# Index logits of the sparse attention: two heads per step, as two 64-row products straight from the rotated tile

## The chip, the cores and the metric

One core of one Trainium2 chip runs the whole program. The metric is the device time of that core in microseconds, as the median of several executions: 2955.22 us over 3 runs (2954.88 to 2957.07).

## The reference, cut to what matters

Two transformer blocks in float32 on 16 + 512 tokens of width 1024. The second block begins with a sparse attention (`dsa_attention`), which picks for every query the 128 keys with the highest index score. Only the score is touched:

```
qi = rope(qi.reshape(B, T, IDX_HEADS, IDX_DIM), cos, sin)     # 8 heads of 64
ki = rope(ki[:, :, None, :], cos, sin)[:, :, 0, :]            # one key head of 64
logits = jnp.einsum('qhd,sd->qhs', qi_blk, ki_s)
score = jnp.einsum('qh,qhs->qs', w_blk, jax.nn.relu(logits))
score = jnp.where(causal, score, -jnp.inf)
_, idx = lax.top_k(score, topk)                               # topk = 128
```

So for each head there is a product of queries and keys over only 64 dimensions, then relu, then a sum over the 8 heads weighted per query.

## The kernel before, in words

Each engine runs its own program, written out by hand; semaphores order them. Tokens are cut into five tiles of 106 (the last of 104), `ROWS` and `ENDS`. Query tile 0 needs no scores, since it has under 128 keys. Query tile t (1 to 4) is scored against the keys 0 to `ENDS[t]`, which are 212, 318, 424 and 528 columns. `pieces` cuts the 528 into two products of 264, since a bank of PSUM holds 512.

The index queries are four tiles of `pf` (12 to 15), each with two heads of 64 rows: head 0 in the partitions 0 to 63 and head 1 in 64 to 127. Tile 16 of `pf` is the index key, with the same 64 rows in both halves (the weights are laid as `[ki, ki]`). All five are rotated in place while the stage `dsa_a` projects them.

The stage around the change comes between two runs of projections, `dsa_a` (8 blocks) and `dsa_b` (10 blocks), and goes through three engines:

- TensorE, `pe_dsa`, lines 1795 to 1810: 32 products, numbered n = 0 to 31. The outer loop is over the four query tiles m, then over the head hh, then over t, so four products of one head follow each other. The moving operand is the key tile with all 128 rows, and the stationary one is a copy of the query tile in which the other head's 64 rows are zero (`ix_zero`). Product n writes the banks 4 and 5 (n even) or 6 and 7 (n odd), and waits for `ix_act`, that is for the relu of product n - 2.
- ScalarE, `act_dsa`, lines 1869 to 1875: for each n the relu from PSUM into `ix_score[n % 2]`. It waits for `ix_pe` (product n) and for `ix_dve` (the sum of n - 2).
- VectorE, `dve_dsa`, lines 1995 to 2004: for each n one SCALAR_TENSOR_TENSOR, which adds the relu times the query's weight to `bias` of tile t. There is a drain ahead of every fourth one, since `bias` of the same t was written four instructions before.

GpSimd makes the copies (`apart`, lines 1908 to 1914): two copies of 64 rows for each query tile, the first two tiles' behind the last weight split of `dsa_a`, the third's and the fourth's when the products of tile m - 2 are through. The other halves were set to zero by four memsets at lines 1921 to 1923. Behind the copies in GpSimd's program stand two `rope_cosine` and then the weight splits of `dsa_b`.

What follows the stage: TensorE's two `spread` products and VectorE's two multiplies with them (line 2008), the rotation of the two key tiles of the attention (`rope_turn`, `rope_cosine`, `rope_sine` 5 and 6), and `dve_topk` on VectorE, sixteen rounds of MAX8 and MATCH_REPLACE8, beside which TensorE, ScalarE and GpSimd do `dsa_b`. A barrier of all engines stands before the attention.

Of the kernel before, what the change touches and what calls it, by code (L numbers as in the profile page):

```python
# [24 lines left out]
P = 128  # L25
# [3 lines left out]
T = NMETA + SEQ  # L29
HT = T // 2  # L30
C = 106
NCH = -(-T // C)
TS = NCH * C
ROWS = [min(C, T - t * C) for t in range(NCH)]
ENDS = [min(C * (t + 1), T) for t in range(NCH)]
# [78 lines left out]
def wait(e, sem, value):  # L114

    if isinstance(value, int) and value <= 0:
        return
    e.wait_ge(sem, value)
# [27 lines left out]
def pieces(n):  # L146

    return [(0, n)] if n <= 512 else [(0, HT), (HT, HT)]


def build_program(nc, io):
# [113 lines left out]
    tmp, half = dsb("free_l", "tmp", [64, 2 * BASE * BASE]), dsb("free_l", "half", [64, BASE * BASE // 4])  # L265
# [13 lines left out]
    pf = r2("pf", [P, 24 * T])  # L279
# [42 lines left out]
    ix_zero = ri("ix_zero", [P, 4, T])  # L322
# [16 lines left out]
    def sem(name):  # L339
        return nc.alloc_semaphore(name)  # L340
# [44 lines left out]
    q_out, q_sq, q_sum, q_turn, q_moved, q_done, q_table = map(sem, (  # L385
        "q_out", "q_square", "q_sum", "q_turned", "q_turned_out", "q_rotated", "q_tables"))
    q_arg, q_root, tok_out, v_turn = sem("q_argument"), sem("q_root"), sem("token_scale_out"), sem("v_turned_dsa")
    ix_q, ix_pe, ix_act, ix_dve = sem("index_q"), sem("index_logits"), sem("index_relu"), sem("index_added")
    f_sq, f_used, f_root, f_inv, f_spread, f_app = map(sem, (
        "fox_square", "fox_square_used", "fox_root", "fox_inverse", "fox_spread", "fox_normalized"))  # L390
    f_turn, f_vturn, f_vout = sem("fox_scale_turned"), sem("fox_v_turned"), sem("fox_v_stored")
# [44 lines left out]
    def tile_at(buf, m, n=T, off=0):  # L436
        step = TS if buf is qkv or buf is oacc else T
        return buf[:, bass.ds(m * step + off, n)]
# [1331 lines left out]
    def pe_dsa(pe):  # L1770
        a0, b0 = SEGS["dsa_a"].b0, SEGS["dsa_b"].b0
        pe.wait_ge(const2_in, 48)
        for j in range(8):
            products(pe, Blk(a0 + j, 0), xah, xal, KT, *((2, None, False, pe_sums(live=True, gained=True))
                                                         if j == 0 else ()))
            if 2 <= j <= 6:
                rope_turn(pe, j - 2)

        pe.wait_ge(rope_dve, 4)
        for c in range(NCH):  # L1780
            pe.transpose(ps[0:ROWS[c], 7, c * 8:(c + 1) * 8], wi[:, c * C:ENDS[c]], ident[0:8, 0:8])
        for c in range(NCH):
            mm = pe.matmul(ps[0:ROWS[c], 7, 64 + c:65 + c], rstd[0:1, c * C:ENDS[c]], ones[0:1, 0:1],
                           start=True, stop=True)
        mm.then_inc(wit_pe, 1)

        pe.wait_ge(rope_dve, 5)
        for m in range(2):
            pe.wait_ge(kn_sq, m + 1)
            for h in range(2):  # L1790
                mm = pe.matmul(ps[0:16, 4 + h, 0:HT], win64[:, 14 - 2 * m:30 - 2 * m],
                               cout[m][:, h * HT:(h + 1) * HT], start=(m == 0), stop=(m == 1))
        mm.then_inc(kn_sum, 1)

        for m in range(4):
            pe.wait_ge(ix_q, m + 1)
            for k in range(IX):
                hh, t = divmod(k, NCH - 1)
                t += 1
                n = m * IX + k  # L1800
                if n == 0:
                    pe.wait_ge(kn_root, 1)
                elif n == 1:
                    pe.wait_ge(tok_out, 1)
                else:
                    pe.wait_ge(ix_act, n - 1)
                for x, (o, c) in enumerate(pieces(ENDS[t])):
                    mm = pe.matmul(ps[0:ROWS[t], 4 + 2 * (n % 2) + x, 0:c], ix_zero[:, 2 * (m % 2) + hh, C * t:ENDS[t]],  # L1808
                                   pf[:, 16 * T + o:16 * T + o + c], start=True, stop=True)
                mm.then_inc(ix_pe, 1)  # L1810

        pe.wait_ge(kn_inv, 1)
        for m in range(2):
            pe.wait_ge(ix_act, 4 * IX - 1 + m)
            for h in range(2):
                mm = pe.matmul(ps[:, 4 + 2 * m + h, 0:HT], spread[:, m * P:(m + 1) * P], hinv[:, h * HT:(h + 1) * HT],
                               start=True, stop=True)
            mm.then_inc(kn_spread, 1)
        rope_turn(pe, 5)
        rope_turn(pe, 6)  # L1820

        def q_turned(m):
            wait(pe, q_moved, m)
            pe.wait_ge(q_out, m + 1)
            for h in range(2):
                mm = pe.matmul(bank(4 + h), rot_q[:, :], tile_at(pf, m, HT, h * HT), start=True, stop=True)
            mm.then_inc(q_turn, 1)
            pe.wait_ge(q_sq, m + 1)
            for c in range(NCH):
                mm = pe.matmul(ps[0:ROWS[c], 6, 16 * c + 2 * m:16 * c + 2 * m + 2], sq[m % 2][:, c * C:ENDS[c]],  # L1830
                               win64[:, 14:16], start=True, stop=True)
            mm.then_inc(q_sum, 1)

        for j in range(10):
            products(pe, Blk(b0 + j, 0), xah, xal, KT)
            if j == 1:
                pe.wait_ge(rope_dve, 7)
                pe.wait_ge(q_table, 1)
            if 1 <= j <= 8:
                q_turned(j - 1)  # L1840
        pe.wait_ge(q_moved, 8)
        for m in range(2):
            pe.wait_ge(q_out, 9 + m)
            for c in range(NCH):
                o = (ps[0:ROWS[c], 4 if m == 0 else 7, c * P:(c + 1) * P] if c < 4
                     else ps[0:ROWS[c], 5 if m == 0 else 2 * (b0 % 2), 0:P])
                at = (10 + m) * T + c * C
                mm = pe.transpose(o, pf[:, at:at + ROWS[c]], ident[:, :])
            mm.then_inc(v_turn, 1)

    def act_dsa(act):
# [15 lines left out]
        act.activation(two(hroot[0:16, :]), pair_of(4, 16), ACT.Sqrt, bias=eps[0:16, 0:1], scale=1.0 / 64  # L1867
                       ).then_inc(kn_root, 1)
        for n in range(4 * IX):
            t = n % (NCH - 1) + 1  # L1870
            w_, rows = ENDS[t], ROWS[t]
            act.wait_ge(ix_pe, n + 1)
            wait(act, ix_dve, n - 1)
            act.activation(as_psum(ix_score[n % 2][0:rows, 0:w_], w_), psum_cols(4 + 2 * (n % 2), rows, w_),
                           ACT.Relu).then_inc(ix_act, 1)
# [29 lines left out]
    def pool_dsa(pool):  # L1905
        a0, b0 = SEGS["dsa_a"].b0, SEGS["dsa_b"].b0

        def apart(m):
            x = tile_at(pf, 12 + m)
            wait(pool, ix_pe, (m - 1) * IX if m > 1 else 0)  # L1910
            pool.drain()
            pool.wait_ge(rope_dve, m + 1)
            pool.tensor_copy(ix_zero[0:64, 2 * (m % 2), :], x[0:64])
            pool.tensor_copy(ix_zero[64:P, 2 * (m % 2) + 1, :], x[64:P]).then_inc(ix_q, 1)

        for j in range(8):
            split_lo(pool, Blk(a0 + j + 1, 0))
            if j == 0:
                pool.wait_ge(const2_in, 48)
                pool.drain()  # L1920
                for i in range(0, 4, 2):
                    pool.memset(ix_zero[64:P, i, :], 0.0)
                    pool.memset(ix_zero[0:64, i + 1, :], 0.0)
                pool.drain()
            if 2 <= j <= 6:
                rope_cosine(pool, j - 2)
            if j == 7:
                apart(0)
                apart(1)
        apart(2)  # L1930
        apart(3)
        pool.drain()
        rope_cosine(pool, 5)
        rope_cosine(pool, 6)

        def q_rotated(m):
            x = tile_at(pf, m)
            t = ix_zero[:, m % 2, :]
            pool.wait_ge(q_moved, m + 1)
            if m == 0:  # L1940
                pool.wait_ge(q_table, 1)
            pool.tensor_tensor(t, t, cossin[:, 1, :], ALU.mult)
            pool.wait_ge(q_sq, m + 1)
            pool.tensor_tensor(x, x, cos_q[:, :], ALU.mult)
            pool.drain()
            pool.tensor_tensor(x, x, t, ALU.add).then_inc(q_done, 1)

        for j in range(10):
            split_lo(pool, Blk(b0 + j + 1, 0))
            if 2 <= j:  # L1950
                q_rotated(j - 2)
        pool.drain()
        zero_halves(pool)

    def dve_dsa(dve):
# [37 lines left out]
        dve.wait_ge(kn_root, 1)  # L1993
        dve.reciprocal(hinv[0:16, :], hroot[0:16, :]).then_inc(kn_inv, 1)
        for n in range(4 * IX):
            hh, t = divmod(n % IX, NCH - 1)
            t += 1
            if n % (NCH - 1) == 0:
                dve.drain()
            head = 2 * (n // IX) + hh  # L2000
            dve.wait_ge(ix_act, n + 1)
            dve.scalar_tensor_tensor(rows_of(bias, t), ix_score[n % 2][0:ROWS[t], 0:ENDS[t]],
                                     wit[0:ROWS[t], t, head:head + 1], rows_of(bias, t),
                                     ALU.mult, ALU.add).then_inc(ix_dve, 1)
        for m in range(2):
            dve.wait_ge(kn_spread, m + 1)
            x = tile_at(pf, 8 + m)
# [840 lines left out]
```

## Time and profile before

| | |
|---|---|
| median of 3 executions | 2955.22 us |
| span of the profiled execution | 2954.3 us (no other time of it is given; the median lies 0.9 us above) |
| TensorE busy | 2750.1 us, 93% of the span |
| VectorE busy | 1457.1 us, 49% |
| granted TensorE clock, mean over the span | 0.969 of full speed |
| first MATMUL to last sum of the index stage | 1515.14 to 1543.75 us |

A MATMUL's recorded time goes from its start until its last result is written, so consecutive ones overlap, and their spacing is shorter than their duration. float32 products run as two LDWEIGHTS and two MATMULs each; the profile has 80 MATMULs of line 1808 for 40 logical products (32, and 8 more because those of 528 columns are cut in two).

### The profile page before, as it was taken

The page shows a single profiled execution, that of the slowest core. Times are in us where ns is not written, and L with a number is a line of the kernel's source. Part 1 is how long each engine was busy: PE and PEld are TensorE (multiplying, and loading weights), DVE is VectorE, ACT ScalarE, POOL GpSimd, SP SyncE. Part 2 cuts the span into 40 slices and gives each one's busy share as a digit, 9 for nine tenths or more (in the row PEclk, how much of TensorE's full clock was granted, in tenths as well). Part 3 has the DMA queues.
Part 4 walks back from the last instruction along what each step waited for, and adds up shares of the span by engine and source line. Part 5 has one row for each costly group of instructions (what it writes and reads, how often), then busy time and mean ns, then how long its engine had stood idle before and what let it go on. Part 6 is the DMA issues. An engine that isn't in the chain of part 4 may idle for free.

```text
span 2954.3 us, 48212 instructions
## 1 busy us (share of the span) xinstructions
PE 2750.1 (93%) x17591; PEld 2406.2 (81%) x17591; DVE 1457.1 (49%) x2316; ACT 1021.6 (35%) x1759; POOL 1097.3 (37%) x588
## 2 busy tenths in 40 slices
PE   6986788889999999999899899999999999999998
PEld 6965788868987778888779679999998988877876
DVE  2664776743212663323679556345366224555433
ACT  4761222223243332222423563222233255422221
POOL 3422333314444444444447003444444310244443
PEclk8997988999999999999999999999999999999999
DMA  3210000012233333333212002232322200133332
GB/s 98 89 50 7 10 10 10 12 52 89 89 92 93 93 94 92 94 93 98 86 36 72 1 1 79 86 90 88 93 86 77 68 30 1 58 92 93 93 93 93
DMA packets 88859, 197.90 MB, mean 67 GB/s; under 512 B 38140, under 2 KB 40238, under 8 KB 88728
## 3 DMA queue, kind: packets, MB, share of 16 engines
q1 hardware_dynamic: 84964, 192.72, 22.0%
q10 hardware_dynamic: 3764, 3.38, 0.4%
q8 instruction: 88, 1.44, 0.2%
q14 instruction: 43, 0.35, 0.0%
HBM read 192.24 MB, written 3.82 MB: 66 GB/s over the span
## 4 chain that ended last, share of the span: by engine, by line
issue 44%; PE 17%; POOL 12%; DVE 4%; ACT 1%; POOLq 1%; DVEq 1%; ACTq 0%
POOL wl L479 12%; PE ps L515 9%; PE ps L2161 2%; PE ps L2192 2%; DVE work L2061 1%; DVE top L2058 1%; PE ps L1808 1%; PE ps L2179 1%; PE ps L2311 1%; PE ps L2320 1%; ACT prob L2230 0%; POOLq L129 0%; DVE rowmax L2261 0%; PE ps L890 0%; PE ps L2164 0%
## 5 line engine op out<-in xcount | busy, mean ns | idle before, releaser
L479 POOL TENSOR_TENSOR wl<-wraw,wh 128x1024 fp32r<-128x1024 f32 x353 | 876.3, 2483 | 1292.7 <-ACT wh L471 1292.6
L471 ACT ACTIVATE wh<-wraw 128x1024 fp32r<-128x1024 f32 x353 | 372.5, 1055 | 578.2 <-PE ps L515 490.3
L515 PE MATMUL ps<-xah,wh 128*128 128x264 f32 (+1 forms) x2672 | 500.5, 328 | 24.7 <-ACT xah L844 14.2
L515 PE MATMUL ps<-xah,wl 128*128 128x264 f32 (+1 forms) x2672 | 488.1, 323 | 0.0
L515 PE MATMUL ps<-xal,wh 128*128 128x264 f32 (+1 forms) x2672 | 486.6, 322 | 0.0
L515 PEld LDWEIGHTS ps<-xah,wh 128*128 128x128 f32 x2672 | 405.6, 189 | 78.7 <-issue 23.8
L515 PEld LDWEIGHTS ps<-xah,wl 128*128 128x128 f32 x2672 | 403.9, 189 | 41.3 <-issue 0.7
L515 PEld LDWEIGHTS ps<-xal,wh 128*128 128x128 f32 x2672 | 402.4, 188 | 40.7
L663 DVE TENSOR_TENSOR res<-res,stage 128x512 f32 (+3 forms) x112 | 81.8, 730 | 440.3 <-ACT stage L579 440.3
L515 PE MATMUL ps<-xbh,wh 128*128 128x264 f32 (+1 forms) x1392 | 274.7, 337 | 13.5 <-POOL wl L479 12.9
L515 PE MATMUL ps<-xbh,wl 128*128 128x264 f32 (+1 forms) x1392 | 270.0, 334 | 0.0
L515 PE MATMUL ps<-xbl,wh 128*128 128x264 f32 (+1 forms) x1392 | 269.5, 333 | 0.0
L515 PEld LDWEIGHTS ps<-xbh,wh 128*128 128x128 f32 x1392 | 218.2, 189 | 48.3 <-POOL wl L479 16.4
L579 ACT ACTIVATE stage<-ps 128x512 f32<-128x512 f32 (+1 forms) x136 | 81.9, 603 | 467.0 <-PE ps L515 466.9
L515 PEld LDWEIGHTS ps<-xbh,wl 128*128 128x128 f32 x1392 | 218.0, 189 | 27.4
L515 PEld LDWEIGHTS ps<-xbl,wh 128*128 128x128 f32 x1392 | 217.5, 188 | 27.4
L656 DVE TENSOR_SCALAR xbh<-stage 128x512 f32 (+3 forms) x102 | 144.7, 1419 | 18.2 <-issue 16.6
L2161 PE MATMUL ps<-pf,qz 128*104 128x264 f32 (+4 forms) x384 | 124.2, 410 | 24.7 <-ACT prob L2230 13.8
L2261 DVE TENSOR_REDUCE rowmax<-ps 106x1 f32<-106x106 f32 (+4 forms) x160 | 77.7, 488 | 126.5 <-PE ps L2166 70.4
L658 DVE TENSOR_TENSOR xbl<-stage,xbh 128x512 f32 (+3 forms) x102 | 116.4, 1141 | 15.3 <-issue 1.5
L1189 PE MATMUL ps<-xq,ob 106*106 106x106 f32 x480 | 64.8, 299 | 61.4 <-DVE xq L1485 41.7
L1189 PEld LDWEIGHTS ps<-xq,ob 106*106 106x106 f32 x480 | 60.1, 211 | 63.8 <-DVE xq L1485 43.4
(332 smaller groups left out, 3250.1 us busy)
## 6 DMA issues: line engine op xcount, KB each, us to landing
wraw<-in_w SPq DMA_DIRECT2D x353, 512.0 KB, 3.5
res<-in_x SPq DMA_DIRECT2D x4, 528.0 KB, 5.8
res<-in_x ACTq DMA_DIRECT2D x1, 2048.0 KB, 7.9
out<-res SPq DMA_DIRECT2D x1, 2048.0 KB, 6.9
block_in<-mt SPq DMA_DIRECT2D x120, 4.0 KB
xq<-block_out SPq DMA_DIRECT2D x120, 8.0 KB
block_out<-yy SPq DMA_DIRECT2D x20, 56.0 KB
cossin<-in_cossin ACTq DMA_DIRECT2D x1, 528.0 KB
```

The source lines that it names most:

```text
L471: act.activation(wh[:, s * DM:(s + 1) * DM], wraw[:, s * DM:(s + 1) * DM], ACT.Copy).then_inc(hi_done, 1)
L479: pool.tensor_tensor(wl[:, s * DM:(s + 1) * DM], wraw[:, s * DM:(s + 1) * DM], wh[:, s * DM:(s + 1) * DM].bitcast(F32), ALU.subtract).then ...
L515: mm = pe.matmul(ps[:, 2 * s + h, 0:width], ws[:, s * DM + kk * P:s * DM + (kk + 1) * P], x[:, at:at + width], start=(h not in [o[0] for o ...
L579: act.activation(shaped(out(j, u), live), acc(b, live=live), func, **more).then_inc(acc_free, 1)
L656: dve.tensor_scalar(hi, x, 1.0, None, ALU.mult)
L658: return dve.tensor_tensor(lo, x, hi.bitcast(F32), ALU.subtract)
L663: return dve.tensor_tensor(r, r, live_stage(u) if live else stage_at(u), ALU.add)
L1189: mm = pe.matmul(out_[:, sl], lhs(r, sl), rhs(r, sl), start=True, stop=True)
L1808: mm = pe.matmul(ps[0:ROWS[t], 4 + 2 * (n % 2) + x, 0:c], ix_zero[:, 2 * (m % 2) + hh, C * t:ENDS[t]], pf[:, 16 * T + o:16 * T + o + c], s ...
L2161: pe.matmul(s, qz[:, 2 * (p % 2) + hh, t * C:ENDS[t]], pf[:, key + o:key + o + c], start=True, stop=False)
L2192: mm = pe.matmul(ps[0:rows, 7, t * 64:(t + 1) * 64], ptr[n % 2][0:ROWS[kb], kb * rows:(kb + 1) * rows], v[0:ROWS[kb], kb, col:col + 64], s ...
L2261: most = dve.tensor_reduce(m, psum_cols(plan["unit", n][0], rows, w_), AX.X if w_ <= 512 else AX.XY, ALU.max, negate=True)
```

## The change

The zeroed copies are gone, with the memsets, the copies and the semaphore `ix_q`. Both heads of a query tile are now computed in one step, for one t: head 0 from the partitions 0 to 63 of the query and the key tile into the banks 4 (and 5), head 1 from the partitions 64 to 127 into the banks 6 (and 7). The step waits once, for `ix_act` >= n with n even, that is until both relus of the step before are done, and its last MATMUL raises `ix_pe` by 2. Each product still is two LDWEIGHTS and two MATMULs, and the order is head 0, head 1 for each piece. The order of n changes with it: m, then t, then the head. ScalarE and VectorE keep their instructions and take t and the head from the new order; VectorE's drain now stands ahead of every second sum, since the two heads of a step add to the same `bias`.

```diff
-        for m in range(4):
-            pe.wait_ge(ix_q, m + 1)
-            for k in range(IX):
-                hh, t = divmod(k, NCH - 1)
-                t += 1
-                n = m * IX + k
-                if n == 0:
-                    pe.wait_ge(kn_root, 1)
-                elif n == 1:
-                    pe.wait_ge(tok_out, 1)
-                else:
-                    pe.wait_ge(ix_act, n - 1)
-                for x, (o, c) in enumerate(pieces(ENDS[t])):
-                    mm = pe.matmul(ps[0:ROWS[t], 4 + 2 * (n % 2) + x, 0:c], ix_zero[:, 2 * (m % 2) + hh, C * t:ENDS[t]],
-                                   pf[:, 16 * T + o:16 * T + o + c], start=True, stop=True)
-                mm.then_inc(ix_pe, 1)
+        pe.wait_ge(kn_root, 1)
+        pe.wait_ge(tok_out, 1)
+        for n in range(0, 4 * IX, 2):
+            m, t = n // IX, n % IX // 2 + 1
+            wait(pe, ix_act, n)
+            for x, (o, c) in enumerate(pieces(ENDS[t])):
+                for hh in range(2):
+                    half = slice(64 * hh, 64 * hh + 64)
+                    mm = pe.matmul(ps[0:ROWS[t], 4 + 2 * hh + x, 0:c], pf[half, (12 + m) * T + C * t:(12 + m) * T + ENDS[t]],
+                                   pf[half, 16 * T + o:16 * T + o + c], start=True, stop=True)
+            mm.then_inc(ix_pe, 2)
```

On ScalarE, GpSimd and VectorE:

```diff
         for n in range(4 * IX):
-            t = n % (NCH - 1) + 1
+            t = n % IX // 2 + 1
...
-        def apart(m):
-            x = tile_at(pf, 12 + m)
-            wait(pool, ix_pe, (m - 1) * IX if m > 1 else 0)
-            pool.drain()
-            pool.wait_ge(rope_dve, m + 1)
-            pool.tensor_copy(ix_zero[0:64, 2 * (m % 2), :], x[0:64])
-            pool.tensor_copy(ix_zero[64:P, 2 * (m % 2) + 1, :], x[64:P]).then_inc(ix_q, 1)
...
-                pool.drain()
-                for i in range(0, 4, 2):
-                    pool.memset(ix_zero[64:P, i, :], 0.0)
-                    pool.memset(ix_zero[0:64, i + 1, :], 0.0)
-                pool.drain()
...
-            if j == 7:
-                apart(0)
-                apart(1)
-        apart(2)
-        apart(3)
-        pool.drain()
...
-            hh, t = divmod(n % IX, NCH - 1)
-            t += 1
-            if n % (NCH - 1) == 0:
+            hh, t = n % 2, n % IX // 2 + 1
+            if hh:
                 dve.drain()
```

## Rows read from the trace of the kernel before

**Rows 1.** The page: its first line.
```profile
span 2954.3 us, 48212 instructions
```

**Rows 2.** Chain that ended last, 1495 to 1560 us: start, length, what.
```profile
1495.68 0.89 PE ps L1752 x4
...
1527.15 2.48 PE ps L1808 x8
...
1530.32 2.48 PE ps L1808 x8
...
1542.31 0.02 issue
...
1542.98 0.77 DVE bias L2002
```

**Rows 3.** Groups by form, 1515 to 1543.8 us: busy us, mean ns, idle before.
```profile
L2002 DVE SCALAR_TENSOR_TENSOR bias<-ix_score,wit,bias 104x528 f32<-104x528 f32 x8 | 6.1, 768 | 3.1 <-ACT ix_score L1874 3.1
...
L1874 ACT ACTIVATE ix_score<-ps 104x528 f32<-104x528 f32 x8 | 4.9, 611 | 3.5 <-PE ps L1808 3.5
...
L2002 DVE SCALAR_TENSOR_TENSOR bias<-ix_score,wit,bias 106x318 f32<-106x318 f32 x8 | 4.4, 547 | 0.2
L1874 ACT ACTIVATE ix_score<-ps 106x424 f32<-106x424 f32 x8 | 4.2, 524 | 3.3 <-PE ps L1808 1.8 <-DVE bias L2002 1.5
L2002 DVE SCALAR_TENSOR_TENSOR bias<-ix_score,wit,bias 106x212 f32<-106x212 f32 x8 | 3.9, 486 | 0.7
L1874 ACT ACTIVATE ix_score<-ps 106x318 f32<-106x318 f32 x8 | 3.5, 437 | 5.3 <-PE ps L1808 5.3
...
L1874 ACT ACTIVATE ix_score<-ps 106x212 f32<-106x212 f32 x8 | 2.7, 342 | 1.2 <-PE ps L1808 1.2
```

**Rows 4.** Timeline inside the stage: start, length, engine, line, instructions [idle before].
```profile
1527.13 1.88 DVE L2002 SCALAR_TENSOR_TENSOR bias<-ix_score,wit,bias 104x528 f32<-104x528 f32 x3 [0.37 <-ACT ix_score L1874]
...
1532.82 0.85 ACT L1874 ACTIVATE ix_score<-ps 104x528 f32<-104x528 f32 x2 [0.42 <-PE ps L1808]
...
1533.49 0.52 PE L1808 MATMUL ps<-pf,ix_zero 128*106 128x318 f32 x1 [0.34 <-ACT ix_score L1874]
```

**Rows 5.** Timeline at the beginning of the stage.
```profile
1515.12 3.44 DVE L1994 RECIPROCAL hinv<-hroot 16x528 f32<-16x528 f32 x1
...
1515.14 0.66 PE L1808 MATMUL ps<-pf,ix_zero 128*106 128x212 f32 x1 [0.88 <-ACT hroot L1867]
...
1518.66 0.90 DVE L2002 SCALAR_TENSOR_TENSOR bias<-ix_score,wit,bias 106x212 f32<-106x212 f32 x2
...
1519.19 0.52 ACT L1874 ACTIVATE ix_score<-ps 106x424 f32<-106x424 f32 x1 [1.50 <-DVE bias L2002]
```

**Rows 6.** Windows: us, busy (instructions) of PE, PEld, DVE, ACT, POOL, clock, DMA, GB/s.
```profile
1509.50:1512.90 3.40, 2.12 (x16) 1.43 (x16) 3.14 (x7) 1.64 (x9) 1.49 (x2) 1.00 0.24 98
1512.90:1516.30 3.40, 2.52 (x7) 1.20 (x6) 3.21 (x7) 0.80 (x2) 0.00 (x0) 0.50 0.00 0
1516.30:1519.70 3.40, 3.40 (x7) 1.72 (x6) 3.16 (x3) 1.18 (x3) 0.00 (x0) 0.50 0.00 0
...
1523.10:1543.60 20.50, 18.45 (x68) 10.29 (x68) 15.79 (x26) 12.12 (x26) 3.48 (x4) 1.00 0.00 1
```

**Rows 7.** Windows of PE alone, elsewhere: us, busy (instructions), clock, DMA, GB/s.
```profile
1724.50:1727.90 3.40, 2.25 (x23) 1.00 0.00 0
```

**Rows 8.** Timeline behind the stage.
```profile
1545.15 2.05 PE L1752 MATMUL ps<-pf,rot 128*128 128x264 f32 x8 [0.99 <-DVE pf L2008]
...
1630.60 0.24 DVE L2022 TENSOR_TENSOR q_scale<-q_scale,tok_scale 106x80 f32<-106x80 f32 x1
...
1632.37 0.66 PE L2161 MATMUL ps<-pf,qz 128*106 128x106 f32 x2 [10.62 <-POOL qz L2134]
```

**Rows 9.** Timeline of GpSimd next to the removed work.
```profile
1461.38 2.40 POOL L479 TENSOR_TENSOR wl<-wraw,wh 128x1024 fp32r<-128x1024 f32 x1 [7.34 <-ACT wh L471]
...
1546.39 2.59 POOL L1758 TENSOR_TENSOR pf<-pf,cossin 128x528 f32<-128x528 f32 x2 [14.84 <-PE ps L1752]
```

More of the change, by code:

```diff
@@ L387, in build_program @@
     q_arg, q_root, tok_out, v_turn = sem("q_argument"), sem("q_root"), sem("token_scale_out"), sem("v_turned_dsa")
-    ix_q, ix_pe, ix_act, ix_dve = sem("index_q"), sem("index_logits"), sem("index_relu"), sem("index_added")
+    ix_pe, ix_act, ix_dve = sem("index_logits"), sem("index_relu"), sem("index_added")
     f_sq, f_used, f_root, f_inv, f_spread, f_app = map(sem, (
```

## The prediction, made blind

> **What bounds the kernel now.** The page comes first: one core, a span of 2954.3 us [rows 1], so that every term below is some 0.1% or less of it per 3 us. The chain of waits is read next, around the changed lines. It runs through this stage: a stretch of eight MATMULs of line 1808 (the products of 318, 424 and 528 columns), then the relu of 528 columns, then the next eight; the stretches begin at 1527.15 and 1530.32, a period of 3.17 us for four products [rows 2]. TensorE works for 2.48 us of it. It needs only two banks free, so it computes one product while ScalarE empties the one before. Both heads of a query tile, eight products, take 6.34 us. VectorE is not the bound there; in the first 4 us it is, since its first sum waits behind a reciprocal until 1518.66, and ScalarE's third relu waits 1.50 us for that [rows 5].
>
> Behind the stage, VectorE's last sum ends at 1543.75 [rows 2]; then its multiplies, the two rotations and the top-k, all of them one chain on VectorE that ends at 1630.84. TensorE, done with `dsa_b`, has then been idle for 10.62 us, until GpSimd's copy behind the barrier [rows 8]. The chain passes from this stage to the attention without slack: each microsecond more or less at the last sum is one at the end.
>
> **What is removed.** Four memsets and eight copies on GpSimd. Behind the memsets GpSimd was idle for 7.34 us before its next weight split, and behind the last copies for 14.84 us before its next rotation [rows 9]. TensorE's waits for the copies show nowhere in the chain [rows 2]. Removing them gives 0. If the copies slowed a sum or two of VectorE beside them, it had idle time there (3.1 us before the sums of 528 columns alone [rows 3]), so again 0.
>
> **What is added: an alternation.** A step has two products into all four banks, and starts when both relus of the step before are done; the relus start when the last MATMUL is done. Nothing of TensorE and ScalarE overlaps any more. One step costs:
> - The relus of both heads. The row of two relus (528 and 212 columns) has 0.85 us where their durations are 611 and 342 ns, so the second starts 0.10 us before the first ends [rows 3, 4]. Two equal ones take 0.58, 0.77, 0.95 and 1.12 us for t = 1 to 4.
> - The handing over. The first relu of the pair ends at 1532.82 + 0.61 = 1533.43 and the MATMUL begins at 1533.49, 0.06 us; MATMUL to relu 0.02 us [rows 2, 4]. The MATMUL behind a wait takes 0.52 us for 318 columns. Streams: four MATMULs of 264 columns in the chain take 0.89 us, so 0.223 us each, 0.179 for 212, 0.268 for 318 and 0.358 for 424. Hence 0.25 us of that 0.52 is weights and pipeline. In all 0.33 us.
> - The MATMULs. No row of this trace has two products in different halves of the rows, so the cost is bounded from both sides: four times the stream if they go one behind the other as all rows here do (0.72, 1.07, 1.43, and eight times 0.223 = 1.78 us), half of that if the two heads run wholly side by side. I take the first, as the row nearest to it: consecutive MATMULs of the same kind [rows 2].
>
> Sums: 1.63, 2.17, 2.71 and 3.23 us, which is 9.74 us for a query tile with both heads, against 6.34.
>
> **VectorE.** Two sums a step, from 0.49 to 0.77 us each. A row of three sums takes 1.88 us, with a drain, where 528, 212 and 318 columns have 0.77, 0.49 and 0.55, so the drain and what is beside it cost some 0.1 us [rows 3, 4]. There are 16 instead of 8. A query tile costs 2 x 2.5 + 4 x 0.1 = 5.4 us, less than 9.7: hidden. It shows once, at the end: the last sum now starts behind the sum and drain before it. That relu of 528 starts 0.51 us before the other, so from the last relu's end it is 0.03 + 0.77 + 0.1 + 0.77 - 0.51 = 1.16 us to the last sum's end; before it was 0.80.
>
> **The start.** TensorE begins at 1515.1, at the low one of the clock's two levels, 1.2 GHz, granted from 1512.9 to 1519.7 [rows 6]. The first MATMUL takes 0.66 us for 0.36 of stream, so the handing over is 0.38. Step 1: 0.38 + 1.43 + 0.58; step 2: 0.38 + 2.14 + 0.77, which ends at 1520.8. The reciprocal's delay is covered by then. Steps 3 and 4 cost 5.94 and end at 1526.7; three query tiles more, 29.2, at 1555.9; the last sum at 1557.1. Against 1543.75 that is +13.3 us.
>
> **The clock.** The granted clock fell after a stretch in which PE was 2.12 of 3.40 us busy, mostly with short products, and stayed low through one with 2.52; it rose after one with 3.40 of 3.40 [rows 6]. At the full clock (2.4 GHz) a later stretch with 2.25 of 3.40 busy kept it [rows 7]. In the new loop the first steps leave gaps of 0.9 us where TensorE was without one from 1516.3 to 1519.7, so the rise may come one stretch of 3.4 us later. Of such a stretch some 70% is streaming at half speed, worth 1.2 us. I add 0.7 of it: +14 us, and since the later chain moves as one piece, 2955.2 + 14 = 2969.2 us (2968.3 against the profiled 2954.3).
>
> **Rivals.**
> *Partly side by side, clock low.* The two MATMULs of a product follow each other in the same rows, so head 1's first can start only with head 0's second: three streams a step instead of four (five instead of eight at t = 4), 0.54, 0.80, 1.07, 1.12 us. That is 8.3 us a query tile at full clock. But TensorE then streams only 3.5 us of it, and from the low level (7.1 of 12.0 us) the clock may stay there, as it did through the stretch with 2.52 of 3.40 us busy. Sum: step 2 ends at 1520.1 (now held by VectorE's second sum), steps 3 and 4 cost 7.2, three tiles 36.0, the tail 1.2: 1564.5, +20.8, and the eight MATMULs of the rotation behind it some 0.9 more: +21.7, 2977 us. For it: the start falls into a low stretch. Against: the stretch with 2.25 busy at full clock.
> *Partly side by side, clock full.* 4.9 + 3 x 8.27 + 1.16 from 1520.1: 1551.0, +7.3, 2962.5 us.
> *Wholly side by side, not slower.* Stream 2.5 us a tile, 7.24 us a tile with all handing over: 4.3 + 22.5 (with 0.3 a tile for the sums, which ScalarE then meets) + 1.16 from 1520.1: 1548.1, +4.4 us, 2959.6, no change that can be told. It decides the sign because the alternation alone, 0.33 x 4 + 3.42 = 4.74, leaves only 1.6 us a tile for the streams before 6.34 is passed; even half of 5.0 is more, so a gain would need a third. With the clock low it is +14.
> *One behind the other, clock low to the end.* 14.9 us a tile: 1575.9, +33 us, 2988.
> *Not what it says:* if the halves' MATMULs wait for each other's results at each change of rows, each step has 0.17 us more per change, some +5 to +8 on the forecast.
>
> The Trainium skill, TensorEngine Tiling (Array Packing), section Key Properties, says that tiles in different rows work independently and load and multiply in parallel; by that rule the rivals side by side hold, and the gain is at most the 2.5 us a tile that their sum has. The same page's section PSUM Bottleneck says that such packing doesn't speed up the emptying of PSUM; that is what the relu rows show here, 3.42 us a tile that nothing overlaps any more. No row of the kernel before can show the first.
>
> **Chances.** One behind the other with the clock mostly full (the forecast, with the added changes of rows) 0.42; partly side by side, low clock 0.25; partly, full clock 0.15; wholly side by side 0.11 (0.06 at full clock); clock low to the end 0.04; something that I don't see and that makes it faster or the same 0.03. The range holds all but the two ends: from wholly side by side at full clock, 2960, to a little beyond the low clock, 2979. A measurement of this kernel tells 0.2%, 5.9 us. Slower by more than that: 0.90. Within it: 0.08 (0.06 for wholly side by side at full clock, and half of the unseen). Faster: 0.02. Both sums are rounded.
>
> **What would show it.** In the profile after, the products' line has steps of both heads in which no MATMUL lies beside a relu, each relu pair behind "PE ps", each MATMUL group behind "ACT ix_score", 9.7 us from one query tile to the next. MATMULs of the second head that start together with those of the first show the rivals; the granted clock of 1519.7 to 1556 tells full from low. GpSimd's idle time grows and nothing moves with it before 1515. The stretch from the last sum to the attention's first MATMUL (88.6 us) stays as long. Wrong is the prediction if this stretch absorbs the delay, or if the period is under 7 us.

## The result, and the profile after

Both kernels ran four times on the same chip. Before: median 2955.59 us (2954.88 to 2957.07). After: median 2972.03 us (2970.16 to 2972.61). The ratio is 1.0055, 95% interval [1.0043, 1.0066]: 16.4 us slower. The profiled execution took 2970.16 us, the lowest of its four; the profiled span grew from 2954.3 to 2968.4 us, so the traces can explain 14.1 us, and the other 2.3 us of the median lie between executions.

The page, first the span and then the engines:

```profile
span 2968.4 us, 48199 instructions
...
PE 2747.9 (93%) x17591; PEld 2399.4 (81%) x17591; DVE 1455.7 (49%) x2316; ACT 1020.6 (34%) x1759; POOL 1088.1 (37%) x576
```

The sign and the size are as forecast (+14); how the loop comes to that time is not. The chain of waits of the kernel after, over one query tile, answers to [rows 2]: start, length, what.

```profile
1528.89 0.04 issue
1528.93 1.77 PE ps L1803 x4
...
1531.15 0.53 ACT ix_score L1869
1531.67 0.04 issue
1531.72 2.11 PE ps L1803 x8
...
1534.36 0.61 ACT ix_score L1869
1534.97 0.04 issue
1535.02 1.06 PE ps L1803 x4
...
1536.35 0.35 ACT ix_score L1869
1536.70 0.04 issue
1536.74 1.42 PE ps L1803 x4
```

This is the alternation of the prediction: MATMULs, both relus, MATMULs, nothing overlapping. But four MATMULs of 424 columns, two for each head, take 1.77 us. The timeline says how they lie, first in a window of 0.03 us, then the whole step:

```profile
1528.93 1.04 PE L1803 MATMUL ps<-pf 64*106 64x424 f32 x2 [0.86 <-ACT ix_score L1869]
...
1528.93 1.75 PE L1803 MATMUL ps<-pf 64*106 64x424 f32 x4 [0.86 <-ACT ix_score L1869]
```

Two MATMULs start within those 0.03 us (their records have 1528.931 and 1528.938), and the second two 0.83 us later, again together. A stream of 424 columns takes 0.36 us at the full clock by the prediction's figures, so 0.72 at the low one: two of them, one behind the other, fit into 1.77 us, four would not. So the two heads run wholly side by side. They do so at half the clock, as the windows show (us, busy and instructions of PE, PEld, DVE, ACT, POOL, clock, DMA, GB/s), which answer to [rows 6]:

```profile
1512.90:1516.30 3.40, 1.79 (x9) 0.53 (x8) 2.25 (x1) 1.28 (x3) 0.00 (x0) 0.91 0.00 0
1516.30:1519.70 3.40, 0.84 (x4) 0.43 (x4) 2.99 (x5) 0.87 (x2) 0.00 (x0) 0.59 0.00 0
1519.70:1557.90 38.20, 24.98 (x79) 10.52 (x76) 18.13 (x29) 13.19 (x29) 0.00 (x0) 0.50 0.00 1
1557.90:1561.30 3.40, 2.54 (x13) 1.88 (x11) 1.47 (x2) 0.00 (x0) 0.90 (x1) 1.00 0.00 0
```

The granted clock falls to its low level, 1.2 GHz, at 1516.9, and comes back at 1557.9. In the kernel before it was at the full level, 2.4 GHz, from 1519.7 on. A query tile takes 10.07 us where it took 6.34.

When the clock fell, TensorE was in its longest wait of the stage. The relus of the second step stood behind VectorE's first sum, and that behind the reciprocal:

```profile
1518.86 1.75 PE L1803 MATMUL ps<-pf 64*106 64x424 f32 x4 [2.71 <-ACT ix_score L1869]
```

The groups by form over the stage, 1515 to 1562 us, answer to [rows 3]: busy us, mean ns, idle time before.

```profile
L1803 PE MATMUL ps<-pf 64*104 64x264 f32 x32 | 8.4, 673 | 4.2 <-ACT ix_score L1869 4.2
...
L1869 ACT ACTIVATE ix_score<-ps 104x528 f32<-104x528 f32 x8 | 4.4, 608 | 8.8 <-PE ps L1803 8.8
```

The relu's duration is what it was (608 against 611 ns), but it waits longer for PE: 8.8 us before the eight relus of 528 columns, where it was 3.5.

The stage in sum: its first MATMUL starts at 1514.07 (before 1515.14) and its last sum ends at 1556.26 (before 1543.75), so it takes 42.19 us instead of 28.61, +13.6. That it begins 1.07 us earlier is not to be put down to the change: GpSimd's weight split ahead of everything that was changed starts 1.30 us earlier already (1426.22 against 1427.52), and a stretch of low clock just ahead of the stage takes some of the lead back. Behind the last sum, the distance to the attention's first MATMUL grew from 88.6 to 90.1, +1.5. Together +14.0, nearly the 14.1 by which the spans differ. So the change itself cost some 15 us in these two executions. The chain shows where the 1.5 comes from:

```profile
1553.99 0.62 ACT ix_score L1869
1554.61 0.14 issue
1554.74 3.58 PE ps L1811 x8
...
1558.35 0.77 DVE pf L1983
```

The eight MATMULs that spread the norms start 1.5 us ahead of the last sum's end, but take 3.58 us at the low clock (before 2.02 at the full one), so VectorE's second multiply waits until 1558.35. The experiments bear this out: the distance is 90.1 to 90.4 us in the four profiles where the clock is still low there, and 88.6 in all others.

### The profile page after: what moved, and what is told of

Same layout as the page of the kernel before. It is cut to its first block, busy times and chain, and to the rows that moved or that the text cites. A ratio compares the mean times of both kernels' runs of the same rounds, so it can differ in the third digit from the quotient of the medians.

```text
span 2968.4 us, 48199 instructions
## 1 busy us (share of the span) xinstructions
PE 2747.9 (93%) x17591; PEld 2399.4 (81%) x17591; DVE 1455.7 (49%) x2316; ACT 1020.6 (34%) x1759; POOL 1088.1 (37%) x576
## 4 chain that ended last, share of the span: by engine, by line
issue 44%; PE 17%; POOL 12%; DVE 4%; ACT 1%; POOLq 1%; DVEq 1%; ACTq 0%
POOL wl L479 12%; PE ps L515 9%; PE ps L2136 2%; PE ps L2167 2%; DVE work L2036 1%; DVE top L2033 1%; PE ps L1803 1%; PE ps L2154 1%; PE ps L2286 1%; PE ps L2295 1%; ACT prob L2205 0%; POOLq L129 0%; DVE rowmax L2236 0%; PE ps L2139 0%; ACT ix_score L1869 0%
## 5 line engine op out<-in xcount | busy, mean ns | idle before, releaser
L515 PEld LDWEIGHTS ps<-xbh,wh 128*128 128x128 f32 x1392 | 218.2, 189 | 48.2 <-POOL wl L479 16.4
```

Source lines behind the costliest of these rows:

```text
L515: mm = pe.matmul(ps[:, 2 * s + h, 0:width], ws[:, s * DM + kk * P:s * DM + (kk + 1) * P], x[:, at:at + width], start=(h not in [o[0] for o ...
```

## The experiments

The loss can lie in the alternation of TensorE and ScalarE, in the half rows or in the clock; each run takes one of these away or puts it back. Diffs are against the kernel after unless another is named. Runs of different chips are compared by their ratios to the kernel before. "Low" and "full" are 1.2 and 2.4 GHz; a period is that of one query tile, eight products of both heads.

### The step alone, with the zeroed copies

The new order and its strict wait, with the zeroed copies of before as stationary operand (and GpSimd's copies back):

```diff
+            if t == 1:
+                pe.wait_ge(ix_q, m + 1)
             wait(pe, ix_act, n)
...
-                    mm = pe.matmul(..., pf[half, (12 + m) * T + C * t:(12 + m) * T + ENDS[t]],
-                                   pf[half, 16 * T + o:16 * T + o + c], start=True, stop=True)
+                    mm = pe.matmul(..., ix_zero[:, 2 * (m % 2) + hh, C * t:ENDS[t]],
+                                   pf[:, 16 * T + o:16 * T + o + c], start=True, stop=True)
```

> The step of two heads with its single wait, but with the zeroed copies (128 rows) of the kernel before, so nothing can lie side by side. Theory A (the price is the alternation of TensorE and ScalarE, and the clock follows from how little TensorE then has to stream): the streams double to 5.0 us a query tile at full clock, TensorE streams half of the time, the clock stays mostly full, the period is 9.7 us a tile and the time 2955.6 + 13 = 2969; with the clock low for good it would be 14.9 us a tile and 2988. Theory B (the halves of rows are themselves slow, and the step costs nothing): near 2956.

Measured: 2975.19 us (2969.93 to 2986.03, four runs), ratio 1.0067 [1.0041, 1.0093]. In its profile the clock is low from 1519.5 to 1526.4, 1529.8 to 1540.0 and 1543.4 to 1550.2; the periods are 13.86, 12.19 and, where the clock is full, 9.80. The last is the 9.74 that the prediction worked out for MATMULs one behind the other. So the alternation was priced rightly, for products of 128 rows. The median is 6 us above theory A's 2969 and the profiled run, at 2976.78, 8 us; the three low stretches explain most of it: the periods of 13.86 and 12.19 are together 6.5 us over two of 9.80. So products of 128 rows, too, lose the clock in this alternation, but they get it back.

### Half rows alone, in the old order

The products of 64 rows in the order, banks and waits of the kernel before: one head's tiles, then the other's (ScalarE and VectorE take the old order back too). Mostly only one half of the rows is at work; where the head changes, the next head's 212 columns lie beside the last 528 of the head before.

```diff
+        for n in range(4 * IX):
+            m, (hh, t) = n // IX, divmod(n % IX, NCH - 1)
...
+                pe.wait_ge(ix_act, n - 1)
+                mm = pe.matmul(ps[0:ROWS[t], 4 + 2 * (n % 2) + x, 0:c], pf[half, ...], pf[half, ...], start=True, stop=True)
+            mm.then_inc(ix_pe, 1)
```

> Products of 64 rows straight from the rotated tile and no copies, but the order and the waits of the kernel before (head by head, each product waiting for the relu of two products ago). Theory A: the period is 3.17 us for four products as before, full clock from the third product on, and the time that of the kernel before within 2 us. Theory B (halves slow, or low clock because only half of the rows works): 2965 or more.

Measured: 2972.48 us (2972.45 to 2974.43, four runs), ratio 1.0055 [1.0038, 1.0072]. Theory A missed by 16 us; theory B had said 2965 or more. The stretch of products of 318, 424 and 528 columns, 2.48 us in [rows 2], takes 4.62 (the x10 counts two MATMULs of the next head's 212 columns, which start inside it):

```profile
1520.64 4.62 PE ps L1806 x10
1525.26 0.60 ACT ix_score L1872
1525.86 0.04 issue
1525.90 4.62 PE ps L1806 x10
```

And the window of the stage (columns as above):

```profile
1524.50:1543.00 18.50, 15.70 (x37) 7.78 (x34) 8.66 (x15) 6.28 (x14) 0.00 (x0) 0.50 0.00 1
```

TensorE is busy for 15.70 of 18.50 us (the seventh experiment has 15.75 in the same window at the full clock), and the clock stays low from 1512.3 to 1560.1. It was low when the stage began, as in the kernel before; there it rose at 1519.7, here it didn't. "Too many gaps" can't be the reason. What differs from the kernel before in the products is the rows alone.

### Filler in the gaps

Full products of 128 rows behind each step, into bank 0, read by nobody; the wait and the heads' products are those of after.

```diff
             mm.then_inc(ix_pe, 2)
+            for _ in range(5 if n == 2 else 1 if t < 3 else 2):
+                pe.matmul(ps[:, 0, 0:HT], ident[:, :], pf[:, 16 * T:16 * T + HT], start=True, stop=True)
```

> The change, with products whose result nobody reads behind each step (one of 264 columns at t = 1 and 2, two at t = 3 and 4, five behind the second step, where ScalarE waits for the reciprocal), all into bank 0 and within TensorE's wait. Theory C (of the 10.07 us a query tile some 2.6 are the low clock): the clock is full again after the first steps, a tile takes 7.3 to 7.5 us, the rows behind the stage are at full clock too, and the time is 2955.6 + 4 to 5 = 2960. Theory D (the clock is low for another reason, or costs little): 2970 to 2973, or more because the added products stand in the way.

Measured: 2960.72 us (2957.14 to 2965.91, ten runs), ratio 1.0017 [1.0007, 1.0026], 11.3 us less than after. The same heads' products in the same steps, with more work behind them, and the loop is faster. Window and chain (the 0.96 and 1.11 us are the heads' products, the 1.09 filler):

```profile
1519.70:1543.00 23.30, 21.23 (x100) 10.38 (x99) 14.30 (x24) 10.76 (x25) 0.00 (x0) 1.00 0.00 1
```

```profile
1526.54 0.96 PE ps L1803 x4
1527.50 1.09 PE ps L1807 x4
1528.59 1.11 PE ps L1803 x8
```

The clock is full, the step of t = 4 takes 1.11 instead of 2.11 us, and the period is 7.61, the price of the alternation when the heads are side by side; the prediction had 7.24 for that, and some 7.5 with the sums that ScalarE then waits for. The filler was in all gaps, also in the 2.7 us behind the second step; which of them it has to be in was not tried.

### A second set of banks

Four more banks, so a step waits only for the relus of the step before the last:

```diff
-            wait(pe, ix_act, n)
+            wait(pe, ix_act, n - 2)
...
-                    mm = pe.matmul(ps[0:ROWS[t], 4 + 2 * hh + x, 0:c], ...
+                    mm = pe.matmul(ps[0:ROWS[t], 4 - 4 * (n // 2 % 2) + 2 * hh + x, 0:c], ...
```

> The change, but every second step writes the banks 0 to 3, free between the two runs of projections, and TensorE waits for the relus of the step before the last. Theory A: TensorE's work goes behind the relus, VectorE's sums are the bound at about 4.9 us a query tile, and the time falls below the kernel before, to about 2950 (2953 if the clock is low and TensorE with 5.0 us of stream plus its waits is the bound). Theory B (halves slow, no matter how they overlap): above 2960.

Measured: 2953.25 us (2951.43 to 2956.06, ten runs), ratio 0.9989 [0.9979, 0.9998]. One stretch of low clock is left, 1521.3 to 1524.7. The period is 5.14, half of that of the kernel after, and the chain is VectorE's:

```profile
1532.61 1.41 DVE bias L1977 x2
1534.02 0.05 DVEq L1974
1534.11 0.78 DVE bias L1977
...
1537.74 1.41 DVE bias L1977 x2
```

### A wait for each head

Head 0's products wait only for head 0's relu, head 1's for head 1's, in the four banks:

```diff
-            wait(pe, ix_act, n)
-            for x, (o, c) in enumerate(pieces(ENDS[t])):
-                for hh in range(2):
+            for hh in range(2):
+                wait(pe, ix_act, n - 1 + hh)
+                for x, (o, c) in enumerate(pieces(ENDS[t])):
...
-            mm.then_inc(ix_pe, 2)
+                mm.then_inc(ix_pe, 1)
```

> The change, but each head's products wait for the relu of their own banks alone, and each head raises the count by itself; all pieces of head 0 come before head 1. Theory A (alternation): head 0 starts when its own banks are free, and ScalarE's relu of head 0 lies beside head 1's products, which saves some 1.5 us of the 10.07 a query tile, 8.5 us a tile at the low clock, about 2966. If the alternation is not what costs: as the change, 2972.

Measured: 2964.74 us (2962.07 to 2966.39, six runs), ratio 1.0032 [1.0020, 1.0045]. The period is 8.53, as theory A had it. The strict wait of the step costs some 7 of the 16 us. The window of the stage shows the clock again:

```profile
1515.00:1546.00 31.00, 30.25 (x72) 14.95 (x72) 16.93 (x29) 13.81 (x29) 0.00 (x0) 0.50 0.00 1
```

TensorE is busy for 30.25 of 31.00 us and the clock is low all the same. The heads' products overlap only in part: of 318 columns, head 0's start at 1530.47 and head 1's at 1531.10, so one half is often alone. That this is the reason is not shown; the stage also began at the low clock, from 1508.9 on.

### Half rows behind a warm engine

The half rows in the old order, with 12 full products ahead of the first, to enter the stage at the full clock:

```diff
                 pe.wait_ge(kn_root, 1)
+                for _ in range(12):
+                    pe.matmul(ps[:, 0, 0:HT], ident[:, :], pf[:, 16 * T:16 * T + HT], start=True, stop=True)
```

> Products of 64 rows in the old order and with the old waits, as in the run before it, but behind twelve full-row products of 264 columns whose result nobody reads, so that the stage begins at the full clock; they delay it by 6 to 8 us. Theory E (a stretch of 64-row products, one after the other, loses the clock by itself): the clock falls again within a few us, the period goes back to 5.26 us for four products, and the time is 2972 or more. Theory F (it only failed to rise because it began low): full clock throughout, a period of 3.17, 2963.

Measured: median 2959.10 us, ratio 1.0027 [1.0010, 1.0044], but of ten runs six lie at 2954.4 to 2959.7 and four at 2971.4 to 2975.3. The profiled one is the highest:

```profile
1522.30:1528.90 6.60, 5.82 (x22) 3.10 (x22) 4.07 (x7) 3.73 (x9) 0.00 (x0) 1.00 0.00 0
1528.90:1560.00 31.10, 27.55 (x59) 13.99 (x60) 14.51 (x24) 10.36 (x24) 0.00 (x0) 0.50 0.00 1
```

Half rows run at the full clock for 6.6 us, with the old pace; then the clock falls, with PE 5.82 of 6.60 us busy, and doesn't come back in the stage though PE is 27.55 of 31.10 us busy. The six lower runs have no profile, but each run's mean granted clock is on record: 0.970 to 0.972 in the six, 0.964 or 0.965 in the four. So half rows don't force the low clock. They risk it, and once low it didn't come back in the stage, here and in the second experiment.

### Zeroed copies with the second set of banks

The zeroed copies of the first experiment with the eight banks of the fourth (`wait(pe, ix_act, n - 2)` and its bank numbers):

```diff
+                    mm = pe.matmul(ps[0:ROWS[t], 4 - 4 * (n // 2 % 2) + 2 * hh + x, 0:c], ix_zero[:, 2 * (m % 2) + hh, C * t:ENDS[t]],
+                                   pf[:, 16 * T + o:16 * T + o + c], start=True, stop=True)
```

> Eight banks as in the faster version, but with zeroed copies of 128 rows, so TensorE streams 5.0 us a query tile at full clock instead of 2.5. Theory G (the gain is from the banks alone, VectorE's sums are the bound at about 5.2 us a tile): 2953 to 2954, as with the halves. Theory H (the halves side by side are needed for it): 2956 or more.

Measured: 2956.68 us (2953.63 to 2958.41, ten runs), ratio 1.0005 [0.9995, 1.0014]. The clock is full from 1520.5 on, and the period 6.26, nearly the 6.34 of before:

```profile
1524.50:1543.00 18.50, 15.75 (x56) 9.09 (x56) 14.26 (x24) 10.21 (x24) 2.65 (x3) 1.00 0.00 1
```

TensorE is busy for 85% of the window. The banks alone give nothing; the halves on top of them give 6.26 - 5.14 = 1.1 us a query tile. Only the two together gain.

### Twins in the other half

The second experiment's kernel, where beside each product of one half goes a twin of the other half, into a bank that nobody reads:

```diff
+                other = slice(64 - 64 * hh, 128 - 64 * hh)
+                mm = pe.matmul(ps[0:ROWS[t], 2 - 2 * hh + x, 0:c], pf[other, ...], pf[other, ...], start=True, stop=True)
```

> The 64-row products in the old order and with the old waits, each with a twin in the other half of the rows (the other head's, into banks 0 to 3, read by nobody), so all 128 rows work while the count of products on the path stays. Theory E (one half of the rows at a time is what keeps the clock low): the twins lie beside the products, the clock rises as in the kernel before, period 3.17 us for four products, 2956, some 16 us less than without twins. Theory I (64-row products are at fault, however many rows work): 2972; or, if twins went one behind the other, 2980 and more.

Measured: 2957.54 us (2955.65 to 2958.13, ten runs), ratio 1.0004 [0.9994, 1.0013]: 15 us less than without the twins, for twice the MATMULs. Window, and two MATMULs of its timeline:

```profile
1524.50:1543.00 18.50, 16.39 (x118) 8.91 (x116) 13.67 (x24) 10.32 (x23) 0.00 (x0) 1.00 0.00 1
```

```profile
1524.15 0.56 PE L1806 MATMUL ps<-pf 64*104 64x264 f32 x1
1524.17 0.55 PE L1809 MATMUL ps<-pf 64*104 64x264 f32 x1
```

The twins start 0.02 us apart and cost nothing that can be told, the period is 6.37, and the clock is full but for 1521.1 to 1524.5. Against 15.70 of 18.50 us at the low clock in the second experiment, PE's busy time is nearly the same. This is the cleanest pair: the same order and waits, and the same banks for what is read; what changes is whether the other half of the rows works too.

### Filler of half rows

The filler of the third experiment with `ident[0:64, :]` and 64 rows of `pf`:

```diff
-                pe.matmul(ps[:, 0, 0:HT], ident[:, :], pf[:, 16 * T:16 * T + HT], start=True, stop=True)
+                pe.matmul(ps[:, 0, 0:HT], ident[0:64, :], pf[0:64, 16 * T:16 * T + HT], start=True, stop=True)
```

> The change with the same filling products behind each step, but of 64 rows instead of 128. Theory E: rows at work are what counts, so this filler does not bring the clock back, and at the low clock it partly stands in the way of the next step: 2974 to 2985. Theory I2 (any work of TensorE in the gaps will do): 2960, as with the filler of 128 rows.

Measured: 2960.78 us (2955.65 to 2973.56, ten runs), ratio 1.0024 [1.0012, 1.0037]. The expectation missed: in most runs filler of one half does as much as full filler (its profile has full clock and the same 7.61), though its spread of 18 us is twice the other's 9. The mean granted clock falls with the time, from 0.972 in the fastest run to 0.963 in the slowest, so it is the clock that some runs lost. So "half rows alone are too little" is too simple a rule when work of both halves lies between.

### The order of the sums

The eight banks, and VectorE's sums in the order t, t + 1 of one head, then of the other, with one drain for four sums (the relus go to four buffers, two of them the freed `ix_zero`):

```diff
-        for n in range(4 * IX):
+        for i in range(4 * IX):
+            n = i - i % 4 + (0, 2, 1, 3)[i % 4]
             hh, t = n % 2, n % IX // 2 + 1
-            if hh:
+            if i % 4 == 2:
                 dve.drain()
...
+    def score_at(n, rows, w_):
+        return ix_score[n % 2][0:rows, 0:w_] if n % 4 < 2 else ix_zero[0:rows, n % 4, 0:w_]
```

> Eight banks with the halves, a ring of four score buffers, and VectorE's sums in the order t, t+1 of head 0 and then of head 1, so that 8 drains stand there instead of 16. Theory A (VectorE is now the bound): each drain costs about 0.18 us from start to start, 1.4 us less, and the stalls at the relu go: 2951 to 2952. If something else is the bound: 2953, as with eight banks.

Measured: 2951.35 us (2949.85 to 2954.87, ten runs), ratio 0.9985 [0.9975, 0.9994]; periods 6.21, 4.69 and 4.69. The same kernel again:

> The same kernel as the one with eight banks, the ring and the new order of sums, for a closer interval: 0.9985 of the kernel before, upper end below 1.

2951.18 us (2947.29 to 2953.46, eleven runs), ratio 0.9982 [0.9973, 0.9991], periods 6.21, 4.69, 4.69: two chips agree, and the second query tile, with 6.21, is the slow one in both. The windows of the second run show the low clock there:

```profile
1515.00:1521.70 6.70, 3.41 (x22) 1.49 (x20) 6.42 (x10) 2.91 (x7) 0.00 (x0) 1.00 0.00 0
1521.70:1528.50 6.80, 6.52 (x24) 3.08 (x24) 5.02 (x9) 4.10 (x11) 0.00 (x0) 0.50 0.00 0
```

### The start filled

The same with six full products behind the fourth step, where TensorE waits for VectorE's reciprocal:

```diff
             mm.then_inc(ix_pe, 2)
+            if n == 6:
+                for _ in range(6):
+                    pe.matmul(ps[:, 5, 0:HT], ident[:, :], pf[:, 16 * T:16 * T + HT], start=True, stop=True)
```

> The version with the ring and the new order of sums, with six full-row products of 264 columns behind the fourth step (into bank 5, read by nobody), where TensorE is idle for 2.5 us because ScalarE and VectorE wait for the reciprocal. In the profile of that version the clock was low from 1521.7 to 1528.5 and the second query tile took 6.21 us instead of 4.69. Theory C (this is the low clock that comes from that idle time): 1.5 us less, 2949.6. If the low stretch has another cause, or VectorE is the bound there too: 2951.

Measured: 2948.22 us (2946.22 to 2951.70, six runs), ratio 0.9970 [0.9958, 0.9982], 9.0 us under the kernel before. It is faster than both kernels. Its windows beside those above:

```profile
1515.00:1521.70 6.70, 6.70 (x28) 4.06 (x29) 6.37 (x8) 3.42 (x8) 0.00 (x0) 0.64 0.00 0
1521.70:1528.50 6.80, 5.54 (x34) 2.72 (x32) 5.37 (x10) 3.73 (x10) 0.00 (x0) 1.00 0.01 2
```

The low stretch now lies at 1513.0 to 1519.8, where VectorE's reciprocal covers it, and the clock is full from then on. The time is as expected, the mechanism only in part: the period that was 6.21 is still 6.00, and from the first sum to the last it is 20.1 us against 20.3. The profiled run is the highest of its six (2951.70, mean granted clock 0.968; the others have 0.970 or 0.971), so how they came lower isn't seen. And the interval overlaps that of the kernel without the six products, so what they add is not shown.

## Why the forecast was near, and where it was wrong

The time came out at +16.4 where +14 was forecast, and that is luck: two terms were wrong, and their errors cancel.

**What bounds the kernel** held: nothing behind the last sum absorbed the delay (12.5 us later there, 14.0 at the copy that opens the attention).

**The removal of the copies is worth nothing.** Held as far as the runs show it: the eighth experiment has the old order and waits without copies and memsets, and stands at the time of the kernel before (1.0004, a period of 6.37 against 6.34). It was not measured by itself.

**The alternation.** Held, and measured twice: 9.80 us a query tile with 128 rows at full clock (forecast 9.74), 7.61 with the halves side by side at full clock (rival: 7.24, and 0.3 for the sums). The handing over of 0.33 us a step was near enough.

**The MATMULs one behind the other.** This is the step that failed. I took four streams a step, "as the row nearest to it", and gave wholly side by side 0.11. Two heads' MATMULs of 64 rows start 7 ns apart, so a step has two streams. Nor does head 1 wait for head 0's second MATMUL, as the rivals "partly side by side" had it. The nearest row was of products that share all rows, and so said nothing of products that share none; the Trainium skill, TensorEngine Tiling (Array Packing), section Key Properties, that tiles in different rows work independently, was the better guide, and the trace agrees: 1.11 us for the step of t = 4 at full clock, against 1.78 of stream alone if its eight MATMULs went one behind the other.

**The clock mostly full.** Failed too, in the other direction. The clock is low for 41 us. With the heads side by side at the low clock the period is 10.07, by chance near 9.74. The miss of the one term, 9.74 - 7.61 = 2.1 us a tile too much, and of the other, 10.07 - 7.61 = 2.5 us too little, cancel. What stood in the rivals as "wholly side by side, with the clock low it is +14" is what happened, number included; its chance, 0.05, was far too small. I reasoned from PE's busy share alone, and [rows 7] with 2.25 of 3.40 us busy at full clock was of products of 104 to 128 rows.

The four tiles then make: alternation at full clock, (7.61 - 6.34) x 4 = 5.1; low clock, (10.07 - 7.61) x 4 = 9.8; together 14.9, where the stage shows 13.6: the first tile lost only 2.4 us and not 3.7, since the kernel before also spent it partly at the low clock. Behind the stage 1.5 more.

**The start.** The prediction took the reciprocal's delay as covered by the second step. It wasn't: TensorE stood for 2.71 us before the third, and in that wait the clock fell.

**Why the clock is low.** Two theories stood: the gaps of the alternation, and the half rows. Filler takes the low clock away, 11.3 us (third experiment), and so does overlap (fourth). But half rows with no more gaps than before have it too, and twins in the other half take it away at the same busy time, 15 us (second and eighth). So in this stage both count: the clock fell and stayed low where only one half of the rows worked, or where both did with gaps of about a microsecond at each step; products of 128 rows with such gaps lost it and got it back (first experiment); and one-half work didn't always lose it (six of ten runs of the sixth experiment, and most with the half-row filler). That PE's busy time alone doesn't tell the clock is shown: at 15.70 of 18.50 us busy it was low, at 15.75 and 16.39 full. What amount of work decides stays open, and so does whether the kernel after would have kept the clock without the 2.71 us at its start.

**VectorE hidden.** Held: 1.16 us from the last relu's end (1555.10) to the last sum's end, as forecast (a drain costs nearer 0.17 than 0.1 us, which changes nothing here). **The stretch behind stays as long** failed by 1.5 us, the spread MATMULs at the low clock; I had priced such a tail only in a rival (0.9 us).

**Not settled.** The median moved by 16.4 us, the profiled span by 14.1. The other three executions of the kernel after have a mean granted clock of 0.962 or 0.963, the profiled one 0.966; where they lost it isn't seen.

## What to carry to other kernels

In a loop like this one, put two products of 64 rows side by side only together with a second set of banks: halves alone gave +16 us, banks alone 0, both -3, with the sums in a better order -5 and with six products more at the start -9 (the last step is within the intervals). Before pricing such a change, price each wait at both levels of the clock, and take products that fill only half of the rows as a risk to the clock that the busy share doesn't show. A forecast that comes out right can be two wrong terms; the period, one MATMUL's start beside its neighbour's, and the granted clock each test one of them.

## What the runs showed of the hardware

- The clock can be low with TensorE busy for 30.25 of 31.00 us, with MATMULs of 64 rows that overlap only in part; and be full with 16.39 of 18.50, with both halves at work.
- Adding MATMULs that nobody reads made the kernel faster, by 11.3 us in the gaps and by 15 as twins.
- MATMULs of two row halves into different banks start 7 ns apart, though head 0's product stands whole ahead of head 1's in TensorE's program: head 1's first MATMUL doesn't wait for head 0's second, which starts 0.83 us later.
- A drain of VectorE between two sums costs some 0.17 us, an estimate from the starts. Without it a sum starts some 0.08 us before the one ahead of it ends (1534.70 after 1534.12 + 0.66 in the last order), with it 0.09 us behind that end (1534.11 after 1533.25 + 0.77 in the fourth experiment). The chain of the last order has sums back to back, and one drain for four:

```profile
1534.12 1.69 DVE bias L1978 x3
1535.81 0.46 DVEq L1975
1536.27 0.09 issue
1536.37 0.91 DVE bias L1978 x2
```

The 0.46 is not the drain's price: the fourth sum runs until 1536.27 beside it. With one drain for two sums the period was 5.14, with one for four 4.69: 0.45 us for two drains fewer and another order of the sums. By the estimate above the drains are some 0.35 of it; the two were not parted.
